# Key chunks first, then value chunks, in the memory and the shared key/value projections of a two-layer encoder step

## The reference, cut to what matters

```
def mem_kv(mem, g_mem, w_mem_kv, k_norm_mem):          # once per layer, 256 memory tokens
    kv = rmsnorm(mem, g_mem) @ w_mem_kv                # 1024 -> 1024 columns
    k = rmsnorm(kv[..., :512] in 4 heads of 128, k_norm_mem)
    v = kv[..., 512:] in 4 heads of 128

def shared_kv(x, g_kv, w_kv, k_norm_fox, b_f):         # once, before layer 1's attention, 576 tokens
    z = rmsnorm(x, g_kv) @ w_kv                        # 1024 -> 1032 columns
    k = rmsnorm(z[..., :512] in 8 heads of 64, k_norm_fox)
    v = z[..., 512:1024] in 8 heads of 64
    logf = log_sigmoid(z[..., 1024:] + b_f)
```

## Time and profile before

| | |
|---|---|
| median of 3 runs | 1389.19 us |
| lowest, highest | 1388.21, 1390.13 us |
| span of the profiled execution | 1383.9 us |
| median less that span | 5.3 us |
| TensorE matmul busy | 1354.2 us (98%) |
| TensorE weight load busy | 1294.2 us (94%) |
| VectorE, ScalarE busy | 601.8 us (43%), 495.3 us (36%) |
| GpSimd busy | 37.2 us (3%) |

### The profile page before, as it was taken

One profiled execution on the slowest core, in us unless ns is written; L12 is line 12 of the kernel. 1 busy time (PEld: TensorE's weight loads), 2 busy tenths in 40 slices (PEclk: granted clock), 3 DMA queues, 4 the chain that ended last, 5 costly groups with the idle time before them and its releaser, 6 DMA issues. The chain is left out here.

```text
span 1383.9 us, 24787 instructions
## 1 busy us (share of the span) xinstructions
PE 1354.2 (98%) x9956; PEld 1294.2 (94%) x9956; DVE 601.8 (43%) x1087; ACT 495.3 (36%) x869; POOL 37.2 (3%) x60
## 2 busy tenths in 40 slices
PE   6999999999999999999999899999999999999997
PEld 6997999999999999999999766699999999999997
DVE  4756444434444433335644454454444434432221
ACT  6556342222222222225743554434222222221221
POOL 1000000000000000011001100000000000000000
PEclk9999999999999999999999999999999999999999
DMA  6332222322223122243343300022232222223231
GB/s 213 98 103 94 59 80 77 90 77 80 87 76 87 54 84 84 83 135 100 120 108 98 108 1 1 1 77 77 77 91 76 84 83 76 83 61 93 92 101 35
DMA packets 202182, 114.31 MB, mean 83 GB/s; under 512 B 5291, under 2 KB 198475, under 8 KB 202120
## 3 DMA queue, kind: packets, MB, share of 16 engines
q1 hardware_dynamic: 198088, 101.24, 25.0%
q0 software_dynamic: 3840, 12.15, 2.4%
q10 hardware_dynamic: 192, 0.06, 0.0%
HBM read 106.54 MB, written 6.90 MB: 82 GB/s over the span
## 5 line engine op out<-in xcount | busy, mean ns | idle before, releaser
L1060 DVE TENSOR_TENSOR WL<-RAW,WH 128x1024 fp32r<-128x1024 f32 (+3 forms) x209 | 233.8, 1118 | 620.8 <-ACT WH L821 620.7
L821 ACT ACTIVATE WH<-RAW 128x1024 fp32r<-128x1024 f32 (+3 forms) x209 | 203.7, 975 | 518.8 <-PE ACCP L1248 518.7
L1248 PE MATMUL ACCP<-XH,WH 128*128 128x288 f32 x1664 | 360.9, 299 | 5.3 <-DVE XL L1064 5.2
L1248 PE MATMUL ACCP<-XH,WL 128*128 128x288 f32 x1664 | 357.6, 297 | 0.0
L1248 PE MATMUL ACCP<-XL,WH 128*128 128x288 f32 x1664 | 357.2, 297 | 0.0
L1248 PEld LDWEIGHTS ACCP<-XH,WH 128*128 128x128 f32 x1664 | 270.0, 190 | 7.5 <-DVE WL L1060 3.8
L1248 PEld LDWEIGHTS ACCP<-XH,WL 128*128 128x128 f32 x1664 | 269.1, 189 | 0.0
L1248 PEld LDWEIGHTS ACCP<-XL,WH 128*128 128x128 f32 x1664 | 269.1, 189 | 0.0
L1248 PE MATMUL ACCP<-HH,WH 128*128 128x288 f32 (+1 forms) x1104 | 238.2, 298 | 0.0
L1248 PE MATMUL ACCP<-HH,WL 128*128 128x288 f32 (+1 forms) x1104 | 236.6, 296 | 0.0
L1248 PE MATMUL ACCP<-HL,WH 128*128 128x288 f32 (+1 forms) x1104 | 236.5, 296 | 0.0
(11 more groups left out here) (220 smaller groups left out, 1068.2 us busy)
## 6 DMA issues: line engine op xcount, KB each, us to landing
RAW<-in_w_gu SPq DMA_DIRECT2D x88, 512.0 KB, 3.7
RAW<-in_w_down SPq DMA_DIRECT2D x32, 384.0 KB, 3.4
RAW<-in_w_down SPq DMA_DIRECT2D x32, 320.0 KB, 3.1
RAW<-in_w_in SPq DMA_DIRECT2D x16, 512.0 KB, 4.0
RAW<-in_w_mem_kv SPq DMA_DIRECT2D x16, 512.0 KB, 3.9
RAW<-in_w_out SPq DMA_DIRECT2D x16, 512.0 KB, 4.1
RAW<-in_w_kv SPq DMA_DIRECT2D x8, 512.0 KB, 3.6
XR<-in_x_prompt SPq DMA_DIRECT2D x4, 512.0 KB, 6.1
```

What stands on the lines that cost most here:

```text
L821: a.activation(WH[:, q % SPLIT_SLOTS, 0:nk, 0:ncol], RAW[:, q % RAW_SLOTS, 0:nk, 0:ncol], ACT.Copy).then_inc(hi_ready, 1)
L1060: v.tensor_tensor(WL[:, q % SPLIT_SLOTS, 0:nk, 0:ncol], RAW[:, q % RAW_SLOTS, 0:nk, 0:ncol], WH[:, q % SPLIT_SLOTS, 0:nk, 0:ncol], ALU.sub ...
L1248: ins_ = t.matmul(ACCP[0:ncol, g % 2, b, 0:c1_ - c0_], w[:, q, k, 0:ncol], m[:, k0 + k, c0_:c1_], start=first and k == 0 and n == 0, stop= ...
```

## The change

The two lists of chunks are put in another order. The memory projection of each layer runs k0 k1 k2 k3 v0 v1 v2 v3 in place of k0 v0 k1 v1 k2 v2 k3 v3, and the shared projection runs gate k0 k1 k2 k3 v0 v1 v2 v3 in place of gate k0 v0 k1 v1 k2 v2 k3 v3. The memory store of layer 1 stays behind the second chunk after the gate, which is now key chunk 1. No instruction is added or removed; all that hangs on a chunk moves with it through the list. SyncE loads the same panels, in the new order.

```
-        for c in [c_ for k in range(HC) for c_ in (k, HC + k)]:
+        for c in range(2 * HC):
             kind = "mk" if c < HC else "mv"
...
-            for c in [2 * HC] + [c_ for k in range(HC) for c_ in (k, HC + k)]:
+            for c in [2 * HC] + list(range(2 * HC)):
                 kind = "fk" if c < HC else ("fv" if c < 2 * HC else "gate")
...
-                if c == HC:
+                if c == 1:
                     store("mem", layer=layer, m=count["job"])
```

## The result

The changed kernel is slower. In the timed runs it has a median of 1390.80 us (1388.72 to 1392.99, 20 runs) against 1387.83 us of the kernel before (1386.51 to 1391.60, 20 runs). The ratio is 1.0018, with a 95% interval of 1.0011 to 1.0024, so plus 2.5 us (the means lie 2.5 us apart, the medians 3.0). Timed once more beside the later experiments, on another chip, it is 1.0024 (1.0015 to 1.0034). The prediction was 1388.5 us, a gain of 0.7. The 1390.80 us lie inside the stated range of 1386.2 to 1391.0, but that is luck: the range was laid around a median of 1389.19 us from three runs, which 20 runs put at 1387.83. Against those three runs its upper end was plus 1.8 us.

The account below looks back on a forecast made before the run. TensorE, executing for 1354.2 of 1383.9 us, was taken as the bound, so only its idle time could be gained. Terms of -0.51, -0.21 and +0.02 gave -0.7 us, from 1389.19 to 1388.5 us, range 1386.2 to 1391.0.

Parts of the forecast that it names:

- Costed at nothing: Work priced at zero, among it loads and, beside the groups, squares, Ln, Exp and scaling of one key per step.
- the first rival: Memory projection: key chain no longer fits a step, turns wait for scaling; chance 0.06 by a tenth, 0.04 by 0.44 us.
- only move: Layer 1's memory projection has no tail, so the norm and turn of k3 change place without a price.
- step 19: Shared projection, behind the cumulative sum: the third job waits 0.31 us for its copy, the same wait before and after.
- Tail of layer 0: Behind the last value chunk of layer 0's memory projection: attention starts 4.07 us after that chunk's issue, 0.82 less.
- E: End of the last chunk's issue ahead of an attention: 110.25 in layer 0, 777.40 in layer 1's shared projection.
- Tail of layer 1: Behind the shared projection's last value chunk: attention 5.03 us after its issue instead of 5.76, copies of k3 gone.
- Layer 0's sum: Layer 0's memory projection: norm of k3 +0.50, stall -0.19, shorter tail -0.82, together -0.51 us.
- Staging buffers: Shared projection, a slower rival: the copy of k2 waits for the store of k0 to land; chance 0.01.
- The small stall ahead of the norm of k2: Memory projections: that norm waits for its squares; made a step earlier, they save 0.19 us in layer 0, 0.21 in layer 1.
- The shared norm: Shared projection: the norm of k3, moved ahead of the last chunk's end, costs 0.75 us; with the tail's -0.73, +0.02.
- Layer 1's sum: Layer 1: -0.21 us in the memory projection from the removed stall, +0.02 us in the shared projection.

Follow-up runs that it names:

- copy_first: The changed kernel, but in the step of value chunk 1 ScalarE copies v0 before it splits the panel: 1.0009 of the kernel before.
- v0_first: The changed kernel with one value chunk ahead of the keys in the memory projection: 1.0000 of the kernel before.
- no_lag: The changed kernel with two sets of squares in the first memory step, so every key's norm and turn come one step earlier: 0.9989 of the kernel before.
- the two filled kernels: The kernel before and the changed kernel, each with idle transposes where TensorE waits: 0.9988 and 1.0002 of the kernel before.
- the third group: Last set of runs on one chip, with 32 executions of the kernel before; the unaltered changed kernel had 1.0024 there.
- mem_only: The kernel before with only the memory projection in the new order, the shared one as before: 1.0018 of the kernel before.

## Why the prediction was wrong

**The step that failed** is in "Costed at nothing" and in the first rival: "the squares, Ln, Exp and scaling of one key per step ... beside the groups". The sums failed with it: layer 0 priced the norm of k3 at 0.50 us wherever it stands, and layer 1 said that it and the turn "only move". I counted work per engine and step, and the turn that waits for a key's scaling. I did not count the jobs per step against the two MISC buffers, so the wait of TensorE for a buffer stood at nothing. I had read that rule in the kernel and used it for step 19, where three jobs stand behind each other, and I took from the lag of the squares a gain of 0.2 us. The same lag puts the norm of k3 into the step of value chunk 1, behind the turns of v0 and k2. Neither of these steps was written out as a list. The before order never has three jobs in a memory step. Cost: 1.25 us in each layer, 2.5 us. Up to layer 1's attention, and without the clock, the profiled spans show plus 2.49 where -0.70 was forecast, 3.19 us apart; the third job is 2.5 of these. copy_first, v0_first and no_lag each take it away in another manner, and each time the loss of 1.04 us per layer shrinks or goes.

**The terms that held.** Tail of layer 0: forecast E + 4.07, measured 4.12. Tail of layer 1: E + 5.03, measured 5.03, with v3's bracket up to 2.74 (forecast about 2.8). Layer 0's sum was -0.51; with the 1.25 added it is +0.74, and 0.86 was measured. The 0.96 us of the split in that count is the distance to the next copy's start; the row has 1.06. Of the 0.9 us of the state's copy the rows shown give no duration. Staging buffers: no wait of L865 for a store; the prompt stores landed in 2.6 to 4.4 us (2.5 to 4.5 before). The copies among the seven operations, of which the prediction spoke there, are casts from fp32 to bf16 (L1144, L1147), and no run shows whether the rule that it quoted covers casts. The small stall ahead of the norm of k2 is gone.

**A term that was too small.** The shared norm was priced by the start of the next instruction, 0.75 us. By step lengths of the changed kernel it is more: a step with only a turn takes 782.93 - 776.00 = 6.93 us, one with two turns 776.00 - 768.51 = 7.49, so a turn is 0.56 and a group 6.37; a step of the kernel before with only a norm takes 769.92 - 762.56 = 7.36. The norm is 0.99 us. Moved from the tail onto the saturated engine it makes the shared projection about 0.26 us slower, not 0.02. The lower price that I quoted from the Trainium skill, "TensorE: Matmul & The Clock Gate", section Back-to-back issue gap, which the page states for an isolated matmul, lies further off: by it four of 288 columns would take an estimated 0.49 us. The measurement decides. Layer 1's sum forecast was -0.19; with 1.25 and 0.24 it is 1.30, and 1.63 was measured. The remaining 0.3 us lie in layer 1's memory projection: from its last query norm to the gates' turn (685.34 to 720.13 before, 688.52 to 724.63 after) the change adds 1.32 us, where 1.25 - 0.21 = 1.04 was due. What they are is open.

**The clock** was not in the forecast at all. I read 1.00 in one execution and took it for the rule. The mean is low in a part of the executions of before too (39 of 102), and in 27 of 30 of the changed kernel. Without it, by the two filled kernels, the change costs 1.0002 - 0.9988 = 0.0014, 1.9 us, each term with an interval of about 0.0009 to either side, and their median spans lie 1.95 us apart (1384.65, 1386.6); with it 2.5 us, or 3.3 in the third group. So the third job is the main cause, and the clock adds some tenths to a microsecond on the median. That idle time in the tails has a part in it is shown by two opposite edits (none of 47 with a low mean where it is filled, 11 of 11 where it is lengthened). It is not the whole rule: mem_only, whose second tail is that of before, has 11 of 12. no_lag, with the tails of the changed kernel, has 2 of 12, but its profiled execution has a fall that the mean doesn't give away. How often the clock falls in each kernel is therefore not known, nor what decides it in the kernels that have the same tails.

**The chances.** The rival "the key chain no longer fits" had the right place (key steps of the memory projection) and the wrong mechanism: the bracket is behind a value's copy, and no turn of a key has one. The 0.88 for "the same" within 0.2% came true only just (1.0018, and 1.0024 when timed again), and by another path. The wrong chance is the 0.77 for the sum as counted: all slower causes together had 0.11, far too little for a change that moves work from idle time onto an engine that is 98% busy.

**A version that beats both.** v0_mem_fill, one value chunk ahead of the keys in the memory projection, the shared order as before, idle transposes in the tails: median 1385.23 us, 0.9981 (0.9972 to 0.9989) of before. Its median span is 1383.6 us against 1385.2, so 1.6 us of the 2.2 between the medians lie inside the span.

## What to carry to other kernels

When a reordering moves jobs that share a small ring of buffers, write out the jobs of every step and count them against the buffers; a job over the ring's depth waits for all that stands ahead of the copy in the emptying engine's queue, here a weight split of 1 us ahead of a copy of 0.4. What lies in an idle tail is free there, and is paid in full once it is moved onto the saturated engine. Price an instruction on TensorE by lengths of whole steps with and without it, not by the gap to its next neighbour.

## What the runs showed of the hardware

Matmuls that compute nothing, in places where TensorE waits anyway, made the kernel before 0.12% faster (0.9988, 0.9979 to 0.9996). With them no profiled execution of four had the half clock in an attention, and none of 47 had a mean clock of 0.994 or less. That this is the whole cause is not shown: 0.67 of the 1.22 us lie outside the span. A wait of 1.15 us more in the same place cost 2.4 us, with the half clock behind it (0.50 and 0.71 over 4 us each).

So an idle stretch of a few microseconds can have a second price behind it, and whether it is paid differs from execution to execution of the same kernel: the changed kernel had the half clock in both attentions in one profile and in layer 1's alone in another. One profiled execution can't show it. The mean clocks of many show a tendency but count no falls, since a fall in layer 1's attention came with a mean of 0.993 in one kernel (mem_only) and of 0.996 in another (no_lag).
